# The recurrence of a hybrid decoder layer: where in a block of 48 tokens the output's products, the next block's scaling and the filler products stand

## The reference

```python
def step(S, inp):
    r_t, w_t, k_t, v_t, kk_t, a_t = inp
    sa = jnp.einsum('bhvk,bhk->bhv', S, -kk_t)
    S = (S * w_t[:, :, None, :] + sa[..., None] * (kk_t * a_t)[:, :, None, :]
         + v_t[..., None] * k_t[:, :, None, :])
    return S, jnp.einsum('bhvk,bhk->bhv', S, r_t)
```

## Time and profile before

| | |
|---|---|
| median of 3 runs | 2023.28 us (2022.06 to 2029.23) |
| profiled execution | 2022.39 us, its span 2020.6 us |
| granted TensorE clock, mean | 0.977 |
| TensorE matmul busy | 1913.2 us (95%) |
| VectorE, ScalarE, GpSimd busy | 1465.7, 759.5, 364.9 us |
| the recurrence, first gram product to the first product of the next stage | 385.99 to 592.42 us |

### The profile page before, as it was taken

The page is one execution under the profiler, slowest core; times in us unless marked ns, Lnnn a source line. Parts: engine busy times, 40 slices in busy tenths (PEclk is TensorE's granted clock), DMA queues, the critical chain, the costliest instruction groups (busy, mean ns, idle before and its releaser), DMA issues. The chain is left out here.

```text
span 2020.6 us, 35186 instructions
## 1 busy us (share of the span) xinstructions
PE 1913.2 (95%) x13873; PEld 1667.3 (83%) x13873; DVE 1465.7 (73%) x3143; ACT 759.5 (38%) x1166; POOL 364.9 (18%) x336
## 2 busy tenths in 40 slices
PE   8999998798989779999999999899779999999999
PEld 8999886577764479999999999899668888888887
DVE  5253334555544256999999999999968888888887
ACT  5322445222222233344334433577523333333332
POOL 2001100400000002133213321000433222322221
PEclk9999998799999989999999999899989999999999
DMA  4222101100021244797679767266979999999996
GB/s 165 85 84 64 52 11 63 54 3 3 3 109 60 80 145 171 281 336 271 238 276 339 273 238 260 72 199 209 304 268 378 340 340 335 345 344 339 336 336 252
DMA packets 175684, 407.25 MB, mean 202 GB/s; under 512 B 16800, under 2 KB 100000, under 8 KB 174752
## 3 DMA queue, kind: packets, MB, share of 16 engines
q1 hardware_dynamic: 132608, 255.96, 37.1%
q0 software_dynamic: 39744, 144.72, 18.9%
q10 hardware_dynamic: 3168, 4.33, 0.6%
HBM read 358.77 MB, written 46.14 MB: 200 GB/s over the span
## 5 line engine op out<-in xcount | busy, mean ns | idle before, releaser
L89 PE MATMUL eo_ps<-vh,e_wh 128*128 128x512 f32 x768 | 300.0, 391 | 11.9 <-DVE e_wl L2009 11.9
L90 PE MATMUL eo_ps<-vh,e_wl 128*128 128x512 f32 x768 | 299.5, 390 | 0.0
L91 PE MATMUL eo_ps<-vl,e_wh 128*128 128x512 f32 x768 | 299.5, 390 | 0.0
L1616 POOL DMA_INDIRECT g_stage<-in_u_rows,gidx x112 | 137.0, 1223 | 704.0 <-DVE gidx L1712 550.8
L1958 ACT CAST vh<-vraw 128x1024 fp32r<-128x1024 f32 x128 | 134.2, 1049 | 315.0 <-PE eo_ps L91 303.1
L1975 POOL DMA_INDIRECT e_rows<-in_v,gidx x128 | 143.8, 1124 | 381.9 <-DVE e_acc_t L1989 344.8
L2000 DVE TENSOR_TENSOR vl<-vraw,vh 128x1024 fp32r<-128x1024 f32 x128 | 156.8, 1225 | 73.6 <-ACT vh L1958 73.2
L89 PE MATMUL h_ps<-x2h,h_uh 128*128 128x384 f32 x520 | 180.8, 348 | 2.5 <-DVE h_ul L1469 2.5
L89 PEld LDWEIGHTS eo_ps<-vh,e_wh 128*128 128x128 f32 x768 | 144.7, 188 | 43.0 <-DVE vl L2000 10.0
L91 PE MATMUL h_ps<-x2l,h_uh 128*128 128x384 f32 x520 | 174.9, 336 | 0.0
L90 PE MATMUL h_ps<-x2h,h_ul 128*128 128x384 f32 x520 | 174.6, 336 | 0.0
(11 more groups left out here) (308 smaller groups left out, 4236.0 us busy)
## 6 DMA issues: line engine op xcount, KB each, us to landing
vraw<-in_v SPq DMA_DIRECT2D x128, 512.0 KB
g_stage<-in_u SPq DMA_DIRECT2D x63, 512.0 KB
e_hid<-HID_scratch SPq DMA_DIRECT2D x128, 192.0 KB
h_uraw<-in_u SPq DMA_DIRECT2D x45, 512.0 KB
wraw<-in_w_z SPq DMA_DIRECT2D x43, 512.0 KB, 3.5
HID_scratch<-h_hid SPq DMA_DIRECT2D x106, 192.0 KB
G_scratch<-g_stage SPq DMA_DIRECT2D x16, 1024.0 KB, 12.4
gm<-G_scratch SPq DMA_DIRECT2D x128, 128.0 KB
```

What stands on the lines that cost most here:

```text
L89: nc.tensor.matmul(out, a[0], b[0], start=start, stop=False)
L90: nc.tensor.matmul(out, a[1], b[0], start=False, stop=False)
L91: return nc.tensor.matmul(out, a[0], b[1], start=False, stop=stop)
L1616: nc.gpsimd.indirect_dma_start(urows[:, j % GBUF_R], None, d["u_rows"], bass.IndirectOffsetOnAxis(ap=gidx[:, j:j + 1], axis=0)).then_inc(r ...
```

## The change

The products of `y` leave level 2: those of pair 0 go between `offs` and `grown` of level 3 of the next block, those of pairs 1 to 3 into the same gap of level 4. VectorE's two scaling parts go from levels 3 and 4 to the gaps of levels 1 and 2, and ScalarE's scaling goes ahead of level 0. `ST` has two buffers and `ar` three, so that `y` can still be formed from the old state. `u` goes from bank 1 to the second half of bank 6, and `y` from bank 7 to the first half of bank 6; with that two TensorE waits go (the gram products no longer wait for `inv` of the block before, and level 2 no longer waits for `nu`), and others take up the banks' new uses. The copy to `yT` goes from level 3 to the end of level 4. The branch products get 28 places: all levels of block 0, levels 0 and 2 of blocks 1 to 10, and three between the last recur's products; 24 are used (empty: level 0 of blocks 0, 2 and 9, level 2 of block 5). The last block forms no `s` and no new state, and the first leaves out the products with the zero state. At the start the zeroing of PSUM is cut to six banks and comes after the two small fills, and ScalarE starts on its exponentials after those two.

```diff
-    SLOTS = 3
+    TURN = ((1, 7), (0, 6), (2, 0))
-        ar = sb("ar", [P, 2, NP4, 2, C])
+        ar = sb("ar", [P, 3, NP4, 2, C])
-        ST = sb("ST", [P, NP4, HD])
+        ST = sb("ST", [P, 2, NP4, HD])
...
                 prepare(c, c % 2)
+                if c < NCH - 1:
+                    scale(c + 1, 1 - c % 2)
                 for lv in range(NLEV):
-                    if lv == 2 and c < NCH - 1:
-                        scale(c + 1, 1 - c % 2)
                     level(c, c % 2, lv)
...
+        SLOTS = [(0, lv) for lv in range(NLEV)] + [(c, lv) for c in range(1, NCH) for lv in (0, 2)] + [
+            (NCH, lv) for lv in range(3)]
+        PIECE_AT = {at: i * EARLY // len(SLOTS) for i, at in enumerate(SLOTS)
+                    if (i + 1) * EARLY // len(SLOTS) > i * EARLY // len(SLOTS)}
...
-            nc.scalar.activation(last[:], L[:, :, bass.ds(C - 1, NCH, step=C)], ACT.Exp).then_inc(started, 1)
-            act.wait_ge(started, 4)
-            scale(0, 0)
+            act.wait_ge(started, 2)
+            scale(0, 0)
             nc.scalar.activation(last[:], L[:, :, bass.ds(C - 1, NCH, step=C)], ACT.Exp).then_inc(started, 1)
...
-            nc.vector.memset(ps[32:64], 0.0).then_inc(started, 1)
+            nc.vector.memset(ex[:, :, 2, :, 0:1], 1.0).then_inc(started, 1)
             nc.vector.memset(ST[:], 0.0).then_inc(started, 1)
-            nc.vector.memset(ex[:, :, 2, :, 0:1], 1.0).then_inc(started, 1)
+            nc.vector.memset(ps[32:64, 0:3], 0.0).then_inc(started, 1)
+            nc.vector.memset(ps[32:64, 4:7], 0.0).then_inc(started, 1)
...
-                if lv >= NLEV - 2 and c < NCH - 1:
-                    scale(c + 1, 1 - b, lv - (NLEV - 2))
+                if lv in (1, 2) and c < NCH - 1:
+                    scale(c + 1, 1 - b, lv - 1)
...
-                if lv == 3:
+                if lv == 3 and c < NCH - 1:
+                    old, new = ST[:, c % 2], ST[:, 1 - c % 2]
                     dve.wait_ge(s_done, c + 1)
+                    if c >= 1:
+                        dve.wait_ge(y_done, c)
+                    nc.vector.tensor_tensor(new, ps[:, 7, 0:256].rearrange("p (a b) -> p a b", a=NP4),
+                                            old, ALU.add).then_inc(s_add, 1)
...
+                if lv == 4:
                     dve.wait_ge(y_done, c + 1)
...
                     nc.vector.tensor_copy(yT[:, :, c * C:c * C + C],
-                                          ps[:, 7, 0:NP4 * C].rearrange("p (a b) -> p a b", a=NP4)).then_inc(y_out, 1)
+                                          ps[:, 6, 0:NP4 * C].rearrange("p (a b) -> p a b", a=NP4)).then_inc(y_out, 1)
...
                 pe.wait_ge(scaled, 4 * c + 3)
                 if c >= 1:
-                    pe.wait_ge(grown_out, c * 2 * NLEV)
                     pe.wait_ge(tok_out, 6 * c)
-                if c >= 2:
-                    pe.wait_ge(u_out, c - 1)
...
-                    if lv == 2 and g == 1 and c >= 1:
-                        pe.wait_ge(u_out, c)
...
-                fox_product(c, lv + 1)
+                if c >= 1 and lv >= 3:
+                    outputs(c - 1, 1 - b, (range(0, 1), range(1, NP4))[lv - 3])
+                fox_product(c, lv)
...
+            def outputs(c, b, pairs):
+
+                mm = sums(6, 0, C, lambda p, f, t: [(ST[f, c % 2, p], ar[f, c % 3, p, 1]),
+                                                    (toks[t, b, 2, p], mk[t, b, p, C:2 * C]),
+                                                    (nu[t, p], mb[t, b, p, C:2 * C])][c == 0:], HD, pairs)
+                if pairs[-1] == NP4 - 1:
+                    mm.then_inc(y_done, 1)
...
+                    if c == NCH - 1:
+                        pe.wait_ge(y_out, c)
...
-                    sums(1, 0, HD, lambda p, f, t: [(inv[t, b, 1, p], rhs[t, p])], C).then_inc(u_done, 1)
+                    sums(6, 256, HD, lambda p, f, t: [(inv[t, b, 1, p], rhs[t, p])], C).then_inc(u_done, 1)
                 if lv == 2:
                     pe.wait_ge(u_out, c + 1)
-                    if c >= 1:
-                        pe.wait_ge(y_out, c)
-                    sums(7, 256, HD, lambda p, f, t: [(toks[t, b, 0, p], toks[t, b, 2, p]), (toks[t, b, 1, p], nu[t, p])],
-                         HD).then_inc(s_done, 1)
-                    sums(7, 0, C, lambda p, f, t: [(ST[f, p], ar[f, b, p, 1]), (toks[t, b, 2, p], mk[t, b, p, C:2 * C]),
-                                                   (nu[t, p], mb[t, b, p, C:2 * C])], HD).then_inc(y_done, 1)
+                    if c < NCH - 1:
+                        sums(7, 0, HD, lambda p, f, t: [(toks[t, b, 0, p], toks[t, b, 2, p]),
+                                                        (toks[t, b, 1, p], nu[t, p])], HD).then_inc(s_done, 1)
+                    if c == NCH - 1:
+                        outputs(c, b, range(NP4))
+                if c == NCH - 1:
+                    fox_product(NCH, lv)
```

More of the change, by code:

```diff
@@ L969, in scale, with fox_copy @@
                 nc.scalar.copy(vt[:, b], zT[:, ZRV:ZRV + 4, t]).then_inc(exps, 1)
-            def fox_copy(c, slot):
-                p = fox_piece(c, slot)
+            def fox_copy(c, lv):
+                p = fox_piece(c, lv)
                 if p is not None and p % PIECES == PIECES - 1:
@@ L977, in prepare @@
             def prepare(c, b):
-                for j, bank in enumerate((6, 7, 0)):
-                    act.wait_ge(turned, 3 * c + j + 1)
+                for n, (j, bank) in enumerate(TURN):
+                    act.wait_ge(turned, 3 * c + n + 1)
                     x = ps[0:C, bank].rearrange("c (p e f) -> c p e f", p=NP4, e=2)
@@ L1052, in recur @@
             def recur(c, b, lv):
-                if lv == 3:
+                if lv == 3 and c < NCH - 1:
+                    old, new = ST[:, c % 2], ST[:, 1 - c % 2]
                     dve.wait_ge(s_done, c + 1)
-                    dve.wait_ge(y_done, c + 1)
[L1056 to L1060, removed]
+                    if c >= 1:
+                        dve.wait_ge(y_done, c)
+                    nc.vector.tensor_tensor(new, ps[:, 7, 0:256].rearrange("p (a b) -> p a b", a=NP4),
+                                            old, ALU.add).then_inc(s_add, 1)
+                    dve.wait_ge(s_add, c + 1)
+                    dve.wait_ge(started, 5)
+                    nc.vector.tensor_tensor(new, new, last[:, :, c:c + 1].broadcast_to([P, NP4, HD]),
+                                            ALU.mult).then_inc(s_out, 1)
+                if lv == 4:
+                    dve.wait_ge(y_done, c + 1)
                     nc.vector.tensor_copy(yT[:, :, c * C:c * C + C],
-                                          ps[:, 7, 0:NP4 * C].rearrange("p (a b) -> p a b", a=NP4)).then_inc(y_out, 1)
+                                          ps[:, 6, 0:NP4 * C].rearrange("p (a b) -> p a b", a=NP4)).then_inc(y_out, 1)
             scale(0, 0, 0)
@@ L1068, in _ @@
         def _(pe):
-            pe.wait_ge(loaded, 48)
             pe.wait_ge(started, 4)
@@ L1092, in prepare @@
                 if c >= 1:
-                    pe.wait_ge(grown_out, c * 2 * NLEV)
                     pe.wait_ge(tok_out, 6 * c)
-                if c >= 2:
-                    pe.wait_ge(u_out, c - 1)
                 for p, f, t in heads():
-                    mm = nc.tensor.matmul(ps[t, 0, p * 96:p * 96 + 96], bt[f, b, p], ar[f, b, p], start=True, stop=True)
+                    mm = nc.tensor.matmul(ps[t, 0, p * 96:p * 96 + 96], bt[f, b, p], ar[f, c % 3, p], start=True, stop=True)
                 mm.then_inc(gram, 1)
@@ L1101, in prepare @@
                 for p, f, t in heads():
-                    mm = nc.tensor.matmul(ps[t, 1, p * 96:p * 96 + 96], kt[f, b, p], ar[f, b, p], start=True, stop=True)
+                    mm = nc.tensor.matmul(ps[t, 1, p * 96:p * 96 + 96], kt[f, b, p], ar[f, c % 3, p], start=True, stop=True)
                 mm.then_inc(gram, 1)
                 for p, f, t in heads():
-                    mm = nc.tensor.matmul(ps[t, 2, p * C:p * C + C], ar[f, b, p, 0], bt[f, b, p], start=True, stop=True)
+                    mm = nc.tensor.matmul(ps[t, 2, p * C:p * C + C], ar[f, c % 3, p, 0], bt[f, b, p], start=True, stop=True)
                 mm.then_inc(gram, 1)
-                if c >= 2:
-                    pe.wait_ge(rhs_out, c - 1)
-                    pe.wait_ge(y_out, c - 1)
-                    pe.wait_ge(s_add, c - 1)
-                for j, (x, bank) in enumerate(((kt, 6), (bt, 7), (vt, 0))):
-                    if j == 2:
+                for j, bank in TURN:
+                    if bank == 7 and c >= 2:
+                        pe.wait_ge(s_add, c - 1)
+                    if bank == 6 and c >= 2:
+                        pe.wait_ge(y_out, c - 1)
+                    if bank == 0:
                         pe.wait_ge(exps, 4 * c + 4)
@@ L1141, in level, with sums @@
                     mm.then_inc(grown, 1)
-            def sums(bank, col, width, terms, rows):
```

(3 more changed lines are left out.)

31 lines of the change are left out of this document (16 added, 15 removed).

## The result

The changed kernel took 1997.63 us (median of 4 runs, 1994.87 to 1999.89) against 2022.67 us of the kernel before (4 runs, the three told of above and one more): a ratio of 0.9864, 95% interval 0.9848 to 0.988, or 25 us less. It is faster by 1.4%. The prediction was 2000 us, range 1994 to 2008.

The account below looks back on a forecast made before the run. TensorE's timeline, with its waits for VectorE and ScalarE, was taken to set the stage; -23.5 us for blocks 1 to 10 with the end and +0.3 for the start gave -23.2, so 2000 us, range 1994 to 2008.

Parts of the forecast that it names:

- rival 1: Whole kernel: the summed terms hold, 2000 us, own range 1996 to 2004; chance 0.66.
- Grams to level 0: Start of each block: kept at 3.43 us, set by VectorE's chain of masks; up to 0.1 a block more possible.
- rival 4: VectorE becomes the bound: scaling does not fit level 1, late `yT` copy delays masks; 9.7 us back, 2010; chance 0.07.
- Level 3: `grown` comes behind `offs` and the first output pair, 0.84 instead of 0.70, so 1.72 us becomes 1.86.
- Level 4: `offs` 0.67 and outputs 1.04 put `grown` at 1.71 us, was 1.59; next grams 0.47 later, was 1.08.
- The products replace a wait: Level 4: 1.04 us of outputs fill TensorE's wait for VectorE's mask, which stands behind the state's update.
- Rival 5: Levels 3 and 4: outputs paid in full, 0.35 and 1.04 us on top; 2012.4; chance 0.04.
- Block 0 and the start: Earlier scaling against more branch products at low clock and scaling beside GpSimd: +0.3 us, bounds -3 and +3.
- The end: From the last `grown` to the closing meeting: 8.4 us, was 7.9; two of three branch products fill ScalarE waits.
- Rival 2: Clock falls oftener: two low stretches back and two more, 4 x 1.7 us; 2007; chance 0.12.
- Rival 3: Clock better: back earlier in block 0 and full at the next stage's start; 3 us less, 1997; chance 0.09.
- Rival 6: Slower than before: TensorE loses its clock for good in the stage; 2024 and above; chance 0.02.

Follow-up runs that it names:

- GpSimd spread: Changed kernel with GpSimd's 16 gate scalings dealt out two a block instead of all at the stage's start; 1994.1 us, ratio to before 0.9826.
- the run with the old places: Changed kernel with the 24 branch products back in the gaps of levels 0, 2 and 4, none behind the last block; 2008.75 us, ratio to before 0.9899.
- outputs two and two: Changed kernel with two pairs of outputs in level 3 and two in level 4, instead of one and three; 1998.67 us, one run.

## Why the prediction was right

It was right, and it is rival 1, the sum, that came: 1997.63 in its own range of 1996 to 2004. Its terms can be held against the rows one by one (what was foretold, then what was measured).
- Grams to level 0 3.43, 3.40; level 0 3.21, 3.22; level 1 1.91, 1.90; level 2 3.25, 3.25. The scaling in level 1 fitted, and rival 4 (VectorE becomes the bound) with it falls: the profile shows it, and moving the scaling back changed blocks 1 to 10 by 0.1 us in all.
- Level 3 1.86, 1.72. I let 0.14 be added for the first pair of outputs; it ended as the mask became ready. Level 4 1.71, 1.62, and 0.47 to the grams, 0.36: small over-estimates of issue distances (16 instructions of `grown` are half of the 0.75 that the earlier trace rows shows for 32). Together 0.37 a block, nearly all of the gap between 163.0 and the measured 159.75 us. So the grams of neighbouring blocks stood 14.63 to 15.47 us apart and not 15.0 to 15.9. Block 1, without the products with the zero state, is 0.73 shorter than its like, 0.74 foretold.
- "The products replace a wait" in level 4 was right only in part. Two runs show the mask ready at 1.32, so 0.30 of the outputs is paid. That the old 1.59 also contained the copy to `yT` was not in the working, which put the whole wait down to the updates of `ST`. Rival 5, which has them paid in full, falls.
- A block's 2.67 us come from: the outputs 1.12, the grams' wait 0.60, `nu`'s wait 0.57 (each put back alone), about 0.27 from the copy to `yT`, read from the rows. The 0.11 that stays has a likely source in the rows: before, the last `inv` sum stood right behind two scaling instructions and started 0.56 after `grown` (457.52 to 458.08), where it starts 0.43 after it with nothing ahead (471.59 to 472.02), and the grams waited for it. No run shows this alone: with the grams' wait gone, the place of the scaling is worth nothing.
- Block 0 and the start were the weak term: +0.3 foretold, +1.5 measured (-1.3 to the first gram, +2.9 in the block), within its bounds. Scaling began 1.5 us earlier and not 1.9, with a load as the last thing waited for (0.52), and from there to the first gram it took 3.9 us instead of 3.7. The collision at level 1 was foreseen at 0.5 and cost 1.14: the branch product that was to cover it took 1.05 at full clock (396.77 to 397.82), where 2.07 had been read from the earlier trace rows at half. Undoing it by either of two means gave the 1.14 back. VectorE's `prepare` in block 0 collides too (1.44 and 1.51 us), which the kernel before had as well and the prediction did not see; with GpSimd spread the way to level 0 is 2.1 us shorter.
- The end: 8.4 from the last `grown`, 8.57 measured; without the three branch products it was 6.32. Between the same starts of the two runs, the first two cost 0.5 us each, half of their 1.06 hidden in the waits for ScalarE, and the third 1.3 with its copy. The prediction had two of them hidden and the third on top.
- The clock of blocks 1 to 10: the sum took both low stretches of the kernel before as gone, and they are, 1.00 in two profiles. They had made the way to level 0 4.85 us in block 5 and 4.70 in block 10 instead of 3.43, so 2.7 us of the gain are the clock. Rival 2, more low stretches, falls with it. In the nine profiles of kernels that have `y` in the gaps, the clock is never low in these blocks, but for 1.6 us at the start of block 1 in the run with the old places; in all three that have `y` in level 2 it is. That is one profile for most kernels, and why it is so is not shown.
- The clock of the start and block 0: low for 20.5 us before, 17.1 now. The first stretch ended 3.4 us sooner, as foretold; a second one of 6.8 us came as it did before. So the 2.9 us by which block 0 is longer are not a worse clock than before, but two more branch products and the collision, at a clock that was still half low. What brings the second stretch is open. It is not TensorE's wait for the collision alone: the kernel before has no such wait at level 1 and had the stretch, in two runs it began before level 1, and with outputs two and two the wait was there and the stretch was not.
- Rival 3: the low 3.4 us at the next stage's start were gone, but what lies behind the stage took the same time (0.1 us apart). Rival 6 falls with the ratio.

So the stage gained 25.2 us where 23.2 were foretold: 3.3 us more in the blocks and the end, and 1.2 less at the start and in block 0. That the two errors have opposite signs is luck, and so is that the profiled execution took 1999.89 us where 1999.2 were foretold: it had spent 2.9 us more ahead of the stage. Not tried alone are the smaller zeroing at the start and the last block's missing `s` and state.

## What to carry to other kernels

In a stage where two engines alternate in short steps, read one period start to start on each engine, and price every edit by where it stands: work that nothing waits for costs its full length behind a step, and only what exceeds the gap if it stands between the question and the answer of the other engine. Look for waits that guard a buffer rather than data (a bank, a state overwritten in place): each of the two gave 0.6 us a period here, `nu`'s for a different bank. A gap can be filled once: a branch product that cost 0.14 us in level 4 cost 1.16 there when the outputs had filled it. Before moving work forward in time, look at what else runs then: the moved scaling met GpSimd's instructions, and a job that nothing waits for (the gates) had to be dealt out to set it free.

## What the runs showed of the hardware that was not expected

- VectorE's scaling instructions, which have two SBUF inputs, took 1.05 to 1.42 us beside GpSimd's 1.26 us instructions and 0.35 us alone, while those that read PSUM kept their length (0.56 for a gram's mask in block 0, as elsewhere). The Trainium skill (SBUF - State Buffer, Who interferes with whom) has it so, and with GpSimd's work spread the same instructions took 0.35 us again.
- The clock made block 0 differ by 2.8 us between two kernels that both have the collision: 22.79 us with 17.1 us of the stage at half speed, 19.98 with 10.2 (outputs two and two). With the collision gone and 10.2 it took 18.96, with GpSimd spread and 6.8 it took 16.82, for the same TensorE instructions.
